# Twenty-four instead of sixteen tokens kept out of the dense expert products of an encoder block

## What is computed

```python
idx = jnp.take_along_axis(cidx.reshape(TB, PH, K * K), pos, axis=-1)
g = jax.nn.softmax(top_s, axis=-1).astype(xb.dtype)
u = expert_u[idx]
a = jax.nn.gelu(jnp.einsum('td,thkd->thk', xb, u), approximate=False)
return jnp.einsum('thk,thkd->td', g * a, expert_v[idx])
```

## Time and profile before

| | |
|---|---|
| median of 3 runs | 966.12 us (965.79 to 967.09) |
| the profiled execution | 965.33 us, its span 963.5 us |
| PE busy | 955.0 us, 99% of the span |
| DVE, ACT, POOL busy | 79%, 58%, 34% |
| HBM traffic | 263 GB/s over the span |

### The profile page before, as it was taken

The page is one execution under the profiler, slowest core; times in us unless marked ns, Lnnn a source line. Parts: engine busy times, 40 slices in busy tenths (PEclk is TensorE's granted clock), DMA queues, the critical chain, the costliest instruction groups (busy, mean ns, idle before and its releaser), DMA issues.

```text
span 963.5 us, 22318 instructions
## 1 busy us (share of the span) xinstructions
PE 955.0 (99%) x7649; PEld 914.3 (95%) x7649; DVE 764.0 (79%) x1607; ACT 557.6 (58%) x995; POOL 331.9 (34%) x201
## 2 busy tenths in 40 slices
PE   9999999999999999999999999999999999999997
PEld 9989899999999999999999999999899899898997
DVE  7988868889799996787777766778777777677776
ACT  6556864666565647677666655555455455454544
POOL 0000000067868778888888880010001000000000
PEclk9999999999999999999999999999999999999999
DMA  8877678766678989999999998999999999999881
GB/s 302 267 228 206 194 200 243 220 192 209 188 232 232 257 224 306 288 266 292 299 270 285 288 273 257 347 333 330 302 318 324 344 293 312 276 311 292 268 257 45
DMA packets 134081, 254.57 MB, mean 264 GB/s; under 512 B 29856, under 2 KB 78880, under 8 KB 133744
## 3 DMA queue, kind: packets, MB, share of 16 engines
q1 hardware_dynamic: 112192, 235.57, 76.9%
q0 software_dynamic: 21376, 17.12, 8.5%
q10 hardware_dynamic: 432, 0.80, 0.2%
HBM read 227.07 MB, written 26.35 MB: 263 GB/s over the span
## 4 chain that ended last, share of the span: by engine, by line
PE 88%; DVE 7%; DMA 3%; issue 1%; ACT 1%; SPq 0%; DVEq 0%; ACTq 0%
PE pOO L1446 40%; PE pSS L1746 9%; PE pOO L1725 7%; PE pTT L1742 6%; PE pMM L1742 6%; PE pOO L1742 6%; PE pOO L1743 3%; PE pMM L1743 3%; PE pTT L1743 3%; DMA raw<-in_stream 2%; DVE wlos L922 1%; PE pSS L1511 1%; PE pSS L1772 1%; PE pSS L1667 1%; PE pTT L1700 1%
## 5 line engine op out<-in xcount | busy, mean ns | idle before, releaser
L658 ACT ACTIVATE whis<-raw 128x1024 fp32r<-128x1024 f32 x326 | 344.7, 1058 | 244.6 <-PE pSS L1746 160.4
L1446 PE MATMUL pOO<-xhi,whis 128*128 128x240 f32 (+1 forms) x1040 | 288.4, 277 | 0.7 <-DVE wlos L922 0.7
L1446 PE MATMUL pOO<-xhi,wlos 128*128 128x240 f32 (+1 forms) x1040 | 285.9, 275 | 0.0
L1446 PE MATMUL pOO<-xlo,whis 128*128 128x240 f32 (+1 forms) x1040 | 285.9, 275 | 0.0
L922 DVE TENSOR_TENSOR wlos<-raw,whis 128x1024 fp32r<-128x1024 f32 x173 | 209.4, 1220 | 26.1 <-ACT whis L658 24.3
L1337 DVE TENSOR_TENSOR wlos<-raw,whis 128x1024 fp32r<-128x1024 f32 x125 | 153.1, 1225 | 81.1 <-ACT whis L658 69.3
L633 POOL DMA_INDIRECT g_scratch<-small x112 | 201.2, 1796 | 40.5 <-issue 33.4
L1446 PEld LDWEIGHTS pOO<-xhi,whis 128*128 128x128 f32 x1040 | 196.3, 189 | 3.3 <-issue 2.0
L1446 PEld LDWEIGHTS pOO<-xhi,wlos 128*128 128x128 f32 x1040 | 196.4, 189 | 0.0
L1446 PEld LDWEIGHTS pOO<-xlo,whis 128*128 128x128 f32 x1040 | 196.3, 189 | 0.0
L594 POOL TENSOR_TENSOR wlos<-raw,whis 128x1024 fp32r<-128x1024 f32 x29 | 69.9, 2416 | 214.4 <-ACT whis L658 214.3
(11 more groups left out here) (297 smaller groups left out, 2009.8 us busy)
## 6 DMA issues: line engine op xcount, KB each, us to landing
raw<-in_stream SPq DMA_DIRECT2D x199, 512.0 KB
raw<-in_vrows SPq DMA_DIRECT2D x128, 512.0 KB
a_scratch<-ast SPq DMA_DIRECT2D x128, 120.0 KB
held<-a_scratch SPq DMA_DIRECT2D x128, 120.0 KB
g_scratch<-ghot SPq DMA_DIRECT2D x32, 256.0 KB, 4.4
held<-x_scratch SPq DMA_DIRECT2D x16, 512.0 KB
held<-g_scratch SPq DMA_DIRECT2D x124, 64.0 KB
biasm<-in_bias SPq DMA_DIRECT2D x8, 256.0 KB, 5.5
```

The source lines that it names most:

```text
L658: act.activation(whi[s], raw[s][:], ACT.Copy).then_inc(hi_ready, 1)
L1446: last = pe.matmul(dst, st, mv, start=(c == 0 and q == 0), stop=(c == len(terms) - 1 and q == 2))
```

## The change

Twenty-four tokens are kept apart, in six sums of four tokens instead of four. `NU` falls from 240 to 232, so all dense matmuls lose 8 moving columns (the wide ones 16), and the gates need 26 steps instead of 28. Sixteen dots stand in the U stage instead of twelve, eight in the V stage instead of four. The tables are written anew, the buffer for the shares grows, and the four gathers that don't fit in the pairs ahead of scatter rounds are issued after the loads of the first gate tiles.

```diff
-G_STEPS = (P - 16) // GTOK
+G_STEPS = (P - 24) // GTOK
-APART = 16
+APART = 24
-DOTS_U = 12
+DOTS_U = 16
-DOT_TILES_U = (49, 55, 65, 68, 79, 84, 92, 97, 105, 111, 119, 124)
+DOT_TILES_U = (49, 55, 65, 68, 79, 84, 92, 97, 104, 109, 112, 115, 118, 121, 124, 126)
-DOT_TILES = (10, 22, 38, 50)
-DOT_GROUPS = (4, 7, 11, 14)
+DOT_TILES = (5, 12, 18, 24, 32, 38, 44, 50)
+DOT_GROUPS = (3, 5, 6, 8, 10, 11, 13, 14)
-ROW_TILES = (2, 9, 16, 23, 33, 39, 45, 51, 57, 63, 69, 75, 81, 87, 93, 99)
-ROUND_TILES = (32, 56, 80, 104)
+ROW_TILES = (2, 7, 11, 15, 25, 29, 33, 36, 41, 45, 48, 52, 57, 61, 65, 68, 73, 76, 80, 84, 89, 92, 95, 98)
+ROUND_TILES = (24, 40, 56, 72, 88, 104)
-        held = sbs(top, "held", [P, 117, NK])
+        held = sbs(top, "held", [P, 125, NK])
             for q in range(4):
                 pool.dma_start(gring[q], g_tiles[q]).then_inc(g_first[q], 16)
+            for j in range(2 * (PH - 2), DOTS_U):
+                gather_u(j)
```

More of the change, by code:

```diff
@@ L277, in build @@
         ysum = xrow[0][:, 0:512]
-        shares = piece(112, 5)[:, 0:SLOT // 2 + APART * SLOT]
+        shares = piece(112, 7)[:, 0:SLOT // 2 + APART * SLOT]
         shares_at = shares[:, SLOT // 2:].rearrange("p (j n) -> p j n", j=GROUPS)[:, :, 0:(PER_GROUP - 1) * (SLOT + 1) + 1:SLOT + 1]
```

## The result

Five runs of the changed kernel have a median of 976.91 us (975.36 to 981.42), five of the kernel before beside it 966.43 us (965.79 to 967.16): a ratio of 1.0112 [1.0098, 1.0126], 10.5 us slower. The forecast was 972.6 us, its range ended at 976.5, and its chance of slower was 0.83. So the sign was right and the size outside the range.

A forecast was written before the change was run, and what follows sets the result against it. PE, busy 99% of the span, was taken as the bound. 965.33 - 5.1 (wide matmuls) + 3.7 (sums) + 5.7 (wait) + 2.2 (clock) = 971.8 us profiled, so a median of 972.6 us, range 967.5 to 976.5.

The forecast's parts named there:

- Narrow matmuls save nothing: Dense matmuls of 240 columns: 8 columns fewer save nothing, since 16 columns cost what 240 do.
- Wide matmuls and gate steps: 768 wide matmuls lose 16 columns each, -5.1 us; two gate steps fewer, -0.96 us, which the wait swallows.
- Two sums: Two more sums of picked rows on PE, 1.85 us each, +3.7 us.
- The wait: End of U stage: gather 12 stands behind the scatter, so dot 12 and tile 121's low part come late, +5.7 us.
- The low clock: After PE's standstill the clock halves for up to 5.2 us of work: 0 to 2.6 us lost, taken as +2.2.
- V transfers at no cost: V stage, tiles 5 to 57: added dots and value gathers need 379 GB/s in all, shortfall inside the reserve, taken as 0.
- the reserve of 8 us: V stage: tiles are ready three ahead of PE, 8 us, enough to cover a transfer shortfall of 2.7 us.
- PE waits 6.7 us and begins tile 121 at 592.4: End of U stage: PE runs dry at 585.7 us, and tile 121 begins at 592.4 against 586.7 before.
- 1 (no low clock): Rival: the wait at tile 121 comes without the low clock, 970.4 us; chance 0.21.
- 2 (the wait covered): Rival: dot 12 runs before DVE is needed, its gather issued by 577 us, 963.7 us, faster; chance 0.09.
- 3: Rival: narrow matmuls do go by columns, 5.1 us less in the V stage, 967.5 us; chance 0.07.
- 4: Rival: transfers miss 372 GB/s, V stage up to 9 us; U stage's crowded end may delay scatter 1 or 2; 975 to 981; chance 0.12.

The follow-up runs named there:

- e8_dots_in_v: Changed kernel, but the U stage keeps the twelve dots and gathers of the kernel before and the V stage makes twelve dots: 965.38 us, ratio 0.9993 to before.
- e1_in_round: Changed kernel with the gathers of dots 12 to 15 issued inside the last scatter round instead of behind it: 968.45 us, ratio 1.0032 to the kernel before.
- e6_filler: Changed kernel with 28 unread matmuls of 128 columns on PE ahead of tile 121: 973.65 us, ratio 1.0071 to the kernel before.
- e5_before_landing: Changed kernel with gathers of dots 12 to 15 issued before the wait for the scatter's landing and the gate tile loads: 971.67 us, ratio 1.0062 to before.
- e3_width: Changed kernel's narrower dense matmuls and 26 gate steps alone, with before's dot, gather and sum tables (eight tokens get no expert output): 960.07 us, ratio 0.9933 to before.

## Why the forecast had the sign and missed the size

**Right.** *Narrow matmuls save nothing*: 111.7 ns before and after. *Wide matmuls and gate steps*: -6.1 against -6.25 us in the medians, though the wide ones by themselves give 4.4 and not 5.1. *Two sums*: 1.85 us each, in the chain. *The wait*: it is where the forecast put it, with the releasers it named, and moving the dots off it (`e8_dots_in_v`) or the gathers ahead of it (`e1_in_round`) removes it. *The low clock*: it came, and filling the wait takes about its price away. *V transfers at no cost*: nearly, 1.35 us in the V stage (1.0 in the 981.42 us execution); the stage runs at 372 to 381 GB/s over 40 us, in the 976.96 us execution

```profile
640.00:680.00 40.00, 40.00 (x278) 37.85 (x277) 32.74 (x65) 20.46 (x31) 4.12 (x4) 1.00 1.04 381
720.00:760.00 40.00, 40.00 (x280) 36.38 (x279) 31.23 (x62) 19.71 (x30) 7.82 (x7) 1.00 1.03 372
```

where before ran at 336 and 339, and PE is busy throughout these two windows: of the reserve of 8 us, reckoned from the earlier trace rows, enough was left. (The forecast counts 13 value gathers at tiles 5 to 57; its table has 12 there. That is 4 GB/s less and changes nothing.)

**The step that failed: "PE waits 6.7 us and begins tile 121 at 592.4".** It began at 595.0, and 600.2 in the other execution, so the wait term of 5.7 us was 8.3 and 13.5. Behind the scatter the step was sound in the 976.96 us execution: from the end of its last transfer to gather 12 the forecast had 6.6 us and the trace has 6.7, the landing 6.6 against 6.0, dot and low part 2.45 against 2.4. What was wrong is the anchor of it all, the scatter's end at 576.7: one sample, and a low one, of a time that came out from 575.2 to 587.9 us. The forecast called it "POOL's own pace" and put bounds round the landing but none round the start of the chain. In the kernel before this spread costs nothing, so neither its times (965.79 to 967.09) nor one profile could show it. The links vary too: from the scatter's end to the restart it is 15.7 us in the forecast, 15.2 and 12.3 in the changed kernel and 17.6 in `e6_filler`, where gather 12 took 7.75 us to land.

**A second term too small: the clock.** The forecast bounded the low stretch at 5.2 us of work and took 2.2 us; it was 6.4 us and 3.1. The bound came from the first matmuls of the kernel, again a single sample: there the records start 0.21 us apart from 1.0 to 5.6 us, the last two of the 24 already at full pace, so the slow stretch is 4.6 us. Behind a wait it was 6.4 us of work here, 6.2 in the 981.42 us execution and 3.4 in `e5_before_landing`. It is no fixed length.

**The miss in sum.** 972.6 to 976.9 us is 4.3 us: 2.6 of the wait, 0.9 of the clock, 0.8 of the V stage. This is the account of one execution, whose time is that of the median; the four others near it were not profiled.

**The rivals.** 1 (no low clock) and 2 (the wait covered) fall with the rows above and the clocks of all five runs. 3 falls with `e3_width`. 4 had its time right, 976.9 lies in its 975 to 981, and its mechanism mostly wrong: in the V stage 1.35 us are lost, not up to 9, and the profiles with the crowded U stage do not end the scatter later. Its smaller half is in part true: in `e1_in_round` the end of the U stage is 3.9 us late. Part of it (gaps of 0.9 and 1.1 us at 553 and 570) is in the changed kernel too, where it made PE run dry at 587.8 instead of 585.7 and so cost nothing behind a wait whose end POOL sets.

**Where the gain went.** Width gives 6.25 us, two sums take 3.7 back: 2.5 us are all that 24 apart can bring. The best placing found loses 1.6 of them again, mostly in the V stage; what is left, about 1 us, is what a measurement of this kernel doesn't tell from nothing.

## What to carry to other kernels

Before a step is hung on an event that nobody waited for until now, ask how much that event moves from one execution to the next: a kernel with slack behind it hides the spread, and one trace shows a single sample of it. Give the start of such a chain a range, not only its links. And price a standstill of PE twice: the time itself, and the matmuls at half clock behind it, which 28 unread matmuls bought back here (3.3 us in the medians).

## What the hardware showed unexpectedly

- The end of 128 indirect transfers in eight chained rounds came anywhere from 575 to 588 us in eleven profiles, 5 and 8 us apart in two executions of the kernel before and of the changed one.
- Behind a gap of 3.2 us (`e5_before_landing`) the clock stood at 0.50 for 3.4 us, and it fell only after PE had resumed its work (at 591.98 us, with PE busy from 591.6). Idle times of PE of 2.3 and 2.4 us differ in what follows: behind the first (`e6_filler`, at 596.55 us) the clock was low, behind the second (`e1_in_round`, at 581.45 us) it stayed up. Why was not tried. The windows behind them, in this order:

```profile
597.70:601.20 3.50, 3.50 (x20) 3.50 (x19) 3.35 (x4) 0.32 (x2) 0.00 (x0) 0.52 0.88 303
```
```profile
581.40:588.00 6.60, 6.55 (x58) 6.58 (x59) 3.59 (x4) 3.10 (x5) 2.61 (x3) 1.00 1.04 322
```

- A matmul with 128 stationary columns cost 110 to 112 ns from start to start with 16, 128, 232 and 240 moving columns. Fewer columns saved time only in the wide ones: 480 to 464 took 5.7 ns off a pair of a wide and a narrow one.
- One core moved 392 to 398 GB/s in windows of 3 to 4 us, and 381 over 40 us, above the 372 in 10 us that the kernel before had shown.
